# Encoder trunk step on one core: keys and values of both branches as one 512-column product, index keys before index queries, index queries in three passes of rounded halves

## What is computed

```python
h = rmsnorm(x, g_attn)
qa, ka, va, qb, kb, vb, iq, ik, iw, ga, gb = split(h @ w_in)   # widths 512,128,128,512,128,128,512,64,8,1024,1024
# branch A: attention over a window of chunks, with sinks
# branch B: attention over the keys that an indexer selects:
dots  = einsum('qhd,sd->qhs', iq, ik)                 # 8 index heads of 64
score = einsum('qh,qhs->qs', iw, relu(dots))
sel   = top_k(score, 128 prompt / 136 sample)         # per query
o     = softmax(qb . kb[sel] + bias) . vb[sel]
```

## Time and profile before

| | us |
|---|---|
| median of three runs | 1030.94 |
| lowest and highest of them | 1030.78, 1036.11 |
| the execution that was profiled | 1036.8 |
| its span on the core | 1035.0 |

### The profile page before, as it was taken

The page is one execution under the profiler, slowest core; times in us unless marked ns, Lnnn a source line. Parts: engine busy times, 40 slices in busy tenths (PEclk is TensorE's granted clock), DMA queues, the critical chain, the costliest instruction groups (busy, mean ns, idle before and its releaser), DMA issues.

```text
span 1035.0 us, 14155 instructions
## 1 busy us (share of the span) xinstructions
PE 925.9 (89%) x5699; PEld 591.2 (57%) x5702; DVE 378.2 (37%) x974; ACT 256.5 (25%) x523; POOL 132.4 (13%) x136
## 2 busy tenths in 40 slices
PE   7989999999999999998999977877887888887996
PEld 7869995456999998994333322322322222234775
DVE  4179996764233436453111101101101011102796
ACT  6244326764323233221000000000000000001542
POOL 2403701113030000001111110011010110000000
PEclk9999998999999999997999999999999899999998
DMA  9850602002834316366999999999999999996601
GB/s 265 118 152 2 203 1 62 1 2 68 263 105 120 78 46 244 128 236 239 427 427 425 427 428 428 424 428 425 429 426 426 427 426 425 427 428 264 254 22 66
DMA packets 60132, 263.72 MB, mean 255 GB/s; under 512 B 11054, under 2 KB 36030, under 8 KB 46224
## 3 DMA queue, kind: packets, MB, share of 16 engines
q1 hardware_dynamic: 54160, 250.99, 63.0%
q0 software_dynamic: 5296, 9.79, 2.6%
q10 hardware_dynamic: 624, 2.23, 0.6%
HBM read 253.99 MB, written 16.85 MB: 262 GB/s over the span
## 4 chain that ended last, share of the span: by engine, by line
PE 63%; DMA 29%; DVE 4%; ACT 2%; issue 1%; SPq 1%; DVEq 0%; ACTq 0%
DMA arena<-in_w_up 25%; PE ps L1111 13%; PE ps L1278 12%; PE ps L980 5%; PE ps L1143 4%; PE ps L1426 4%; PE ps L1303 3%; PE ps L881 3%; PE ps L952 3%; DMA arena<-in_w_ple 2%; PE ps L1044 2%; PE ps L1014 2%; PE ps L1065 2%; PE ps L1399 1%; PE ps L1172 1%
## 5 line engine op out<-in xcount | busy, mean ns | idle before, releaser
L1278 PE MATMUL ps<-arena,hT 128*64 128x512 f32 x960 | 234.5, 641 | 39.4 <-DMA arena<-in_w_up 39.2
L1278 PEld LDWEIGHTS ps<-arena,hT 128*64 128x64 f32 x960 | 71.6, 141 | 199.3 <-issue 149.4
L2211 DVE TENSOR_TENSOR xf<-xf,ps 128x256 f32<-128x256 f32 x32 | 13.5, 421 | 401.6 <-ACT xf L1699 379.1
L1111 PE MATMUL ps<-arena_merge,arena_merge 128*128 128x256 f32 x624 | 99.7, 287 | 0.0
L1303 PE MATMUL ps<-arena,xf 128*64 128x512 f32 x336 | 76.7, 598 | 12.8 <-DVE xf L2214 12.8
L1111 PEld LDWEIGHTS ps<-arena_merge,arena_merge 128*128 128x128 f32 x624 | 87.4, 188 | 0.0
L836 POOL DMA_INDIRECT expert_rows<-xf,arena x32 | 32.2, 1007 | 425.6 <-ACT xf L1703 399.8
L1111 PE MATMUL ps<-xf_merge,arena_merge 128*128 128x256 f32 x480 | 82.0, 288 | 0.0
L1699 ACT ACTIVATE xf<-ps 128x256 f32<-128x256 f32 x30 | 11.6, 385 | 259.1 <-PE ps L1278 259.1
L1111 PEld LDWEIGHTS ps<-xf_merge,arena_merge 128*128 128x128 f32 x480 | 69.3, 188 | 0.0
L1703 ACT ACTIVATE xf<-ps 128x512 f32<-128x512 f32 x30 | 17.9, 598 | 159.8 <-PE ps L1303 159.8
(11 more groups left out here) (309 smaller groups left out, 1311.1 us busy)
## 6 DMA issues: line engine op xcount, KB each, us to landing
arena<-in_w_gate SPq DMA_DIRECT2D x30, 2048.0 KB, 29.4
arena<-in_w_up SPq DMA_DIRECT2D x30, 2048.0 KB, 37.0
arena<-in_w_down SPq DMA_DIRECT2D x11, 2048.0 KB, 36.4
hT<-in_w_down SPq DMA_DIRECT2D x11, 2048.0 KB, 36.5
arena<-in_w_down SPq DMA_DIRECT2D x20, 1024.0 KB, 32.2
arena<-in_w_in SPq DMA_DIRECT2D x10, 1024.0 KB, 6.2
arena<-in_w_in SPq DMA_DIRECT2D x3, 2048.0 KB, 10.5
arena<-in_w_gate SPq DMA_DIRECT2D x8, 512.0 KB, 9.0
```

The lines of the kernel that those rows point to most:

```text
L1111: mm = pe.matmul(w[:, 2 * lo_t:lo_t + hi_t], rounded(st[:, c, cols]), rounded(mv[:, c, lo_t:hi_t]), start=c == 0 and k == 0, stop=c == pla ...
L1278: mm = pe.matmul(ps[g * BLK:(g + 1) * BLK, 2 + s, :], xsT[:, c, col:col + BLK], expert_columns(k, slice(0, 2), c, g), start=c == 0, stop=c ...
```

## The change

1. **Order of loads.** The weights of `ikw` are loaded before those of `iq`, the bucket table and the bias table after them; two of the three gain vectors move behind the constants. A's keys and values weights are loaded as soon as `ikw` has been computed, ahead of the `toeplitz` write.
2. **Index keys first.** PE computes `ikw` ahead of `iq`. The bias table and the two `ikT` transposes stand between the groups of `iq`.
3. **Index queries in three passes.** `iq` weights are split (high halves `iq_hi` by ACT; low halves by DVE for m = 0, 1 and by POOL for m = 2, 3), and each group is 48 products of rounded halves in place of 16 in float32. They wait for `hT_f` and `hT_lo`.
4. **Keys and values at once.** The weights of A and B lie side by side (`kv_hi2`, `kv_lo2`), and each token tile is one set of 8 x 3 products of 512 columns (256 of A, 256 of B). ACT empties each tile by two copies. `sums` comes after all five tiles, and then the transposes of both branches' keys.
5. ACT makes the high halves of the `qb` weights before it empties the keys and values, no longer after B's.

```diff
 WIDE, WIDE_DONE = ring(
-    [(('xT', t), 'dve') for t in range(TILES)] + [(('iq', m), 'dve') for m in range(4)]
-    + [(('ikT', s), 'dve') for s in 'ps']
+    [(('xT', t), 'dve') for t in range(TILES)] + [(('iq', 0), 'dve'), (('ikT', 'p'), 'dve'), (('iq', 1), 'dve')]
+    + [(('ikT', 's'), 'dve'), (('iq', 2), 'dve'), (('iq', 3), 'dve')]
...
 NARROW, NARROW_DONE = ring(
-    [('table', 'dve')] + [(('ikw', t), 'dve') for t in range(TILES)]
-    + [(('kvb', t), 'act') for t in range(TILES)] + [(('kva', t), 'act') for t in range(TILES)], 2)
+    [(('ikw', t), 'dve') for t in range(TILES)] + [('table', 'dve')]
+    + [(('kv', t), 'act') for t in range(TILES)], 2)
...
# SP
+        sp.wait_ge(narrow_full, NARROW[('ikw', 4)].fill)
+        load(slab_kva, w_in[:, :, C_KVA:C_KVA + 256], slab_in['kva'])
 
         sp.wait_ge(tabp_ready, 1)
         load(toep_d, tab[0:16, :].unsqueeze(1).to_broadcast([16, P, DIST]), toep_moved)
 
         sp.wait_ge(wide_full, WIDE[('iq', 3)].fill)
         load(slab[0], w_in[:, :, C_QB:C_QB + 512], slab_in['qb'])
-        sp.wait_ge(wide_full, WIDE[('ikT', 'p')].fill)
-        load(slab_kva, w_in[:, :, C_KVA:C_KVA + 256], slab_in['kva'])
-        sp.wait_ge(narrow_full, NARROW[('kva', 4)].fill)
+        sp.wait_ge(narrow_full, NARROW[('kv', 4)].fill)
         load(slab[1], w_in[:, :, C_QA:C_QA + 512], slab_in['qa'])
...
# POOL
-        pool.wait_ge(tabp_ready, 1)
         for c in range(KD):
             pool.wait_ge(f_high, c + 1)
             low_of(hT_lo[:, c, :], hT[:, c, 0:NT], hT_f[:, c, :]).then_inc(f_split, 1)
-        pool.wait_ge(sw_high, 1)
+        for m in (2, 3):
+            pool.wait_ge(sw_high, m + 1)
+            low_of(slab[0][:, :, m * P:(m + 1) * P], slab[0][:, :, m * P:(m + 1) * P], iq_hi[m], "front").then_inc(sw_split, 1)
+        pool.wait_ge(sw_high, 5)
         low_of(slab_kvb, slab_kvb, kv_hi['b'], "front").then_inc(sw_split, 1)
+        pool.wait_ge(sw_high, 6)
+        low_of(slab_kva, slab_kva, kv_hi['a'], "front").then_inc(sw_split, 1)
...
# PE
+        def index_queries(m):
+            w = wide(open_slot(WIDE, ('iq', m), wide_out))
+            pe.wait_ge(sw_high, m + 1)
+            for k in range(3):
+                if k == 2:
+                    pe.wait_ge(*((iq_split, m + 1) if m < 2 else (sw_split, m - 1)))
+                for c in range(KD):
+                    if m == 0 and k < 2:
+                        pe.wait_ge((f_high, f_split)[k], c + 1)
+                    st = slab[0][:, c, m * P:(m + 1) * P] if k == 2 else iq_hi[m][:, c, :]
+                    mv = hT_lo if k == 1 else hT_f
+                    for a in range(2):
+                        mm = pe.matmul(w[:, a * 512:a * 512 + HALF], rounded(st, "front"),
+                                       rounded(mv[:, c, a * HALF:(a + 1) * HALF]),
+                                       start=c == 0 and k == 0, stop=c == KD - 1 and k == 2)
+            mm.then_inc(wide_full, 1)
...
-        pe.wait_ge(wide_out['dve'], WIDE[('ikT', 's')].out)
+        pe.wait_ge(wide_out['dve'], WIDE[('iq', 3)].out)
...
+        pe.wait_ge(sw_split, 4)
+        for t in range(TILES):
+            slot = open_slot(NARROW, ('kv', t), narrow_out)
+            for c in range(KD):
+                for k, (st, mv) in enumerate(((hT_f, kv_hi2), (hT_f, kv_lo2), (hT_lo, kv_hi2))):
+                    mm = pe.matmul(by_half(ps[0:ROWS[t], 6 + slot, :]), rounded(st[:, c, tok(t)]), rounded(mv[:, :, c, :], "front"),
+                                   start=c == 0 and k == 0, stop=c == KD - 1 and k == 2)
+            mm.then_inc(narrow_full, 1)
+        w = wide(open_slot(WIDE, 'sums', wide_out))
+        pe.wait_ge(relu_used, 3 * HEADS + KV)
+        for lo, hi in ((0, PAST), (PAST, PAST + NS)):
+            mm = pe.matmul(w[0:NS, lo:hi], ident_s, score_s[:, lo:hi], start=True, stop=True)
+        mm.then_inc(wide_full, 1)
+        pe.wait_ge(narrow_out['act'], NARROW[('kv', 4)].out)
+        for br, kv_n in (('b', kv_b), ('a', kv_a)):
...
# ACT, behind the relus
+        act.wait_ge(slab_in['qb'], 16)
+        query_weights_high(slab[0], qb)
+        for t in range(TILES):
+            slot, r = close(NARROW, ('kv', t), narrow_full), ROWS[t]
+            act.activation(kv_b[0:r, t, :], ps[0:r, 6 + slot, 256:512], ACT.Copy)
+            act.activation(kv_a[0:r, t, :], ps[0:r, 6 + slot, 0:256], ACT.Copy).then_inc(narrow_out['act'], 1)
```

More of the change, by code:

```diff
@@ L901, in _ @@
             mm.then_inc(wide_full, 1)
[L903 to L908, removed]
+        pe.wait_ge(slab_in['ikw'], 16)
         pe.wait_ge(wide_out['dve'], WIDE[('xT', 4)].out)
[L910 to L913, removed]
         for t in range(TILES):
@@ L945, in _ @@
         pe.wait_ge(f_split, KD)
-        for br, s, c_k, kv_n in (('b', slab_kvb, cb_k, kv_b), ('a', slab_kva, None, kv_a)):
-            pe.wait_ge(sw_split, 'ba'.index(br) + 1)
-            for t in range(TILES):
-                slot = open_slot(NARROW, ('kv' + br, t), narrow_out)
-                for c in range(KD):
-                    for k, (st, mv) in enumerate(((hT_f, kv_hi[br]), (hT_f, s), (hT_lo, kv_hi[br]))):
-                        mm = pe.matmul(ps[0:ROWS[t], 6 + slot, 0:256], rounded(st[:, c, tok(t)]),
-                                       rounded(mv[:, c, :], "front"), start=c == 0 and k == 0, stop=c == KD - 1 and k == 2)
-                mm.then_inc(narrow_full, 1)
-            if br == 'b':
-                w = wide(open_slot(WIDE, 'sums', wide_out))
-                pe.wait_ge(relu_used, 3 * HEADS + KV)
-                for lo, hi in ((0, PAST), (PAST, PAST + NS)):
-                    mm = pe.matmul(w[0:NS, lo:hi], ident_s, score_s[:, lo:hi], start=True, stop=True)
-                mm.then_inc(wide_full, 1)
+        pe.wait_ge(sw_split, 4)
[13 more added lines that the diff above has]
+        for br, kv_n in (('b', kv_b), ('a', kv_a)):
             w = wide(open_slot(WIDE, ('k' + br + 'T', 'p'), wide_out))
-            pe.wait_ge(narrow_out['act'], NARROW[('kv' + br, 4)].out)
             for t in range(4):
@@ L1901, in _ @@
                               rounded(ik_hi[:, lo:lo + cols], "front").bitcast(F32), ALU.subtract).then_inc(wide_out['dve'], 1)
+        index_queries(0)
+        dve.wait_ge(consts_ready, 1)
+        slot = close(NARROW, 'table', narrow_full)
+        dve.tensor_copy(tab[0:16, :], ps[0:16, 6 + slot, 0:DIST]).then_inc(narrow_out['dve'], 1)
+        dve.wait_ge(narrow_out['dve'], NARROW['table'].out)
+        link(dve.tensor_tensor(nrm[0:16, 31:32], tab[0:16, 0:1], nrm[0:16, 30:31], ALU.mult))
+        dve.tensor_scalar(tab[0:16, :], tab[0:16, :], nrm[0:16, 31:32], -1.0, ALU.subtract, ALU.mult).then_inc(tabp_ready, 1)
+        index_keys(0, 'p', 0, NP)
+        index_queries(1)
+        index_keys(1, 's', NP, PAST + NS)
+        dve.memset(msk, 0.0)
+        index_queries(2)
+        index_queries(3)
         dve.wait_ge(narrow_out['dve'], NARROW_DONE['dve'])
```

109 lines of the change are left out of this document (55 added, 54 removed).

## The result

| us | before | after |
|---|---|---|
| median of four runs each | 1033.07 | 1050.68 |
| lowest and highest | 1030.78, 1036.11 | 1050.10, 1052.44 |
| the execution that was profiled | 1036.8 | 1050.64 |
| its span | 1035.0 | 1048.8 |

The ratio is 1.0158, with a 95% interval of 1.013 to 1.0186: the change makes the kernel slower by 1.6%, where 0.6% were forecast. (The ratios in this text are estimates with an interval, not quotients of the medians beside them; here the medians lie 17.6 us apart, 1.7%.) Between the two profiled executions it is +13.8 us, where the sum said +6.6; the profiled execution of the kernel before, at 1036.8, was longer than all four that its median is taken from. The sign is right, and so is the new wait; the size is not.

The account below looks back on a forecast made before the run. The front looked bound by PE, with DVE 0.7 us behind it. -3.6 (index part) + 10.1 (DVE's wait) - 0.7 (DVE's lead) + 0.8 (clock) = +6.6, taking the median from 1030.94 to 1037.5; range 1033 to 1042.

Parts of the forecast that it names:

- the sum: Start of attention: -3.6 index part, +10.1 DVE wait, -0.7 DVE's lead, giving +5.8; +0.8 for the clock, +6.6 us in all.
- Part 1: Index keys and queries on PE up to the dots: keys 8.23 us, queries 24.26; dots start at 58.1, 3.6 us earlier.
- halves: Rounded high and low halves for the index queries, made by ACT, POOL and DVE: in time, cost put at nothing.
- the wait for the last group: Ahead of the dots, PE waits until the last group of `iq` is split: 2.9 us with the signal.
- Part 2: Dots: DVE sets the pace, unchanged; they end 3.6 us earlier, PE at 76.0 and DVE's first round at 78.3.
- Part 3: Keys and values on PE: 120 products of 512 columns take 27.3 us, gaining 1.4, but `sums` is delivered only at 104.4.
- rival (d): DVE's wait for `sums` vanishes because 512-column products are quick; attention at 157.8, 4.3 us gained, 1026.6; chance 0.05.
- rival (b): PE later still at keys and values, `qb` rounding delaying ACT (cover 3 us) or halves late; taken as 3 us, 1040.5; chance 0.10.
- (d)'s two limits: Keys-and-values product times: at most 144 ns for the wait to vanish; at 181 ns the attention's start stays where it is.
- Part 4: DVE stands still for `sums` from 94.3 to 104.4, a new 10.1 us wait; attention starts at 167.9, 5.8 us later.
- Part 5: Clock at the attention's head after PE's 12 us idleness: block 0 +0.8 us, block 1 stays at the low level as now.
- Rival (a): The clock recovers early, at 2.4 GHz by attention block 1, giving back its 2.6 us: +3.2, 1034.1; chance 0.20.

Follow-up runs that it names:

- Dense work ahead of it: The changed kernel with eight 128-column identity products, results unused, on PE between the transposes of x and the index keys; 1043.81, ratio 1.0094.
- `sums` early: The changed kernel with the two `sums` products moved into the keys-and-values loop, behind its second tile; 1040.34, ratio 1.0029.
- the index part alone: The changed kernel with keys and values taken back to two times 120 products of 256 columns, `sums` between them; 1037.07, ratio 1.0025.
- dense work in the middle: The changed kernel with 16 identity products on PE behind the first tile of the index keys; 1049.43, ratio 1.0159.
- the versions with seven products: Seven identity products before attention: changed kernel with `sums` early and eight ahead of index keys, 1027.66; that with old keys and values, 1030.86; kernel before, 1033.12.

## Why the prediction was right in sign and short in size

- **Index keys, Part 1: wrong, and this is the step that failed.** "Index keys cost as before 8.23 us" took a row that was measured at 2.4 GHz behind dense work and moved it behind light transposes and a wait. It cost 15.96, +7.7 us, and this went through dots, `sums` and DVE to the attention undiminished: the dots began 6.7 us after the forecast (7.7 less the 1.4 that PE began earlier, plus 0.4 of index queries). Dense work ahead of it brings 8.38; the rest of part 1 holds. The profile of before had the warning. The window in which PE makes the same transposes (columns as above) has a mean granted clock of 0.83, so a part of it was at the low level; windows of 2 us put this at about 15 to 18, and the clock was back before the index queries began:

```profile
10.00:20.00 10.00, 7.54 (x51) 7.15 (x50) 8.77 (x26) 6.46 (x8) 0.00 (x0) 0.83 1.06 337
20.00:30.00 10.00, 10.00 (x43) 7.83 (x42) 2.85 (x7) 7.53 (x11) 7.97 (x7) 1.00 0.80 171
```

  The clock was looked at where it had cost before, not where the change put a new first product.
- **Index queries, halves, the wait for the last group: right.** 24.70 us for 24.26, and 2.90 for 2.9. Nothing of PE waited for a half of `iq`.
- **Dots, Part 2: right** in that nothing of it changed.
- **Keys and values, Part 3: right.** 27.99 us for 27.3, 233 ns a product, like the dearer of the two rows. The Trainium skill's page "TensorE: Matmul & The Clock Gate", section "Back-to-back issue gap", gives 131 ns; this trace does not agree, and rival (d) was out with it. Of (d)'s two limits, 144 ns follows from its sum; by the same sum the copy is as late as before at 173 ns and the attention at 179, not 181, which changes nothing in the forecast. The cover of rival (b) held: the `qb` weights landed at 86.4, 7 us later than thought, yet ACT was free by 90.7, and PE ran its 120 products in one piece.
- **The wait of DVE, Part 4: right.** 10.74 us for 10.1; `sums` early takes it away. PE stood idle for 13.96 us ahead of the attention where 12 were forecast. Behind it DVE needed 1.0 us more than the 63.2 of before, all of it in one instruction (below).
- **The clock at the attention, Part 5: right in direction, mis-sized beneath.** Block 0 took +0.6 for +0.8, block 1 +0.9 where none was expected. But the price of the low clock in block 1 was read as 11.1 - 8.5 = 2.6 us, with block 2 as the likeness. Block 1 itself takes 7.1 at the full clock: the price is 4 us before, and 4.8 after. Rival (a), which gives this price back, was undersized by 1.3 us.
- **Sum.** Between the profiles 7.2 us were missing (13.8 for 6.6). The attention came 8.5 us later than forecast: 6.7 from the dots, 0.7 from keys and values, 1.0 from DVE's mask. Its first two blocks took 0.7 more, the rest up to the merge 0.3; 2.2 were given back behind it, where the sum had expected nothing.
- **The range** ended at 1042 and the median was 1050.7, 13.2 us above the forecast of 1037.5. Of these, 7.2 are the missing ones just named, 2.1 are that the median of before is 1033.07 with its fourth execution and no longer 1030.94, and 3.8 that the medians lie further apart (17.6) than the profiles. With the index keys at 8.23 us the median would have been about 1043 (with the identity products ahead of them 1043.81 was measured), still just outside: their price is the largest part, but not all of it.

What stays open: why the clock falls at about 18.6 in one execution, at 19.1, 21.0 or 23.4 in others with almost the same work ahead (the index part alone; dense work in the middle; `sums` early), and in some, by their times, not at all; and whether it is the wait or the light transposes ahead of it that lets it fall, as the identity products filled the one and stood behind the other. Nor is it settled what else scatters the kernel before and the versions with seven products.

## What to carry to other kernels

A duration of PE is good only with the granted clock of its window: before moving a stretch of products to the head of a stage, look at what PE does just ahead of that place and at the granted clock there, and put its price at 1.2 GHz beside that at 2.4: here 15.96 and 8.23 us. When a reduction that another engine waits for stands behind a loop, merging two loops puts it behind both; what the merge gains is lost in that wait, unless the reduction moves into the loop. And where a PE wait ahead of critical work can't be removed, a few dense products in it can be worth more than they cost, but have to be looked at over several executions.

## What the runs showed of the hardware

- In the kernel after PE was 2.00 of 2.00 us busy with the 72-column products from 20 to 34, at a granted clock of 0.50. With identity products among them the clock came back at about 27.8 while these ran, with PE as busy as before; it stayed at 1.00 under the narrow products that followed, while with `sums` early it fell to 0.50 in the midst of them.
- DVE's mask instruction of block 2 took 1.37 us in place of 0.36. It began at 132.63 and ended at 134.00, and POOL was in an instruction from 132.50 to 133.79. The mask before, and POOL's instruction after:

```profile
118.62 0.36 DVE L1944 TENSOR_SCALAR arena<-hT 128x384 bf16<-128x384 f32 x1
...
132.50 1.29 POOL L768 TENSOR_TENSOR arena_front<-arena,arena_front 128x512 fp32r<-128x512 f32 x1
```

  In the three experiments that kept DVE's wait, this mask met POOL's work and took 1.17 to 1.45 us; in those without it, and in before, DVE passed the place before POOL began, and it took 0.36. DVE's selection beside the same work of POOL did not lengthen (0.56 us for each search for the largest). A delay of one engine can move it into another's way. The Trainium skill's page "Advanced Engine Details and Errata", section "Mode Summary", says that two-port VectorE instructions and GpSimd instructions block each other, since they share a port. The trace agrees for the mask; which mode it ran in, no view shows.
